# Input projections of a two-layer decoder trunk computed as three one-pass products of high and low parts

## The chip, the cores and the metric

The kernel runs on one core of a Trainium2 chip. The metric is the device time of one execution in microseconds. Three runs of the kernel before took 1989.72, 1990.03 and 1991.49 us; the median is 1990.03 us.

## The reference, cut to what matters

576 tokens (512 of a prompt, 64 of eight short decoding sequences) go through two layers. All numbers are 32-bit floats.

```
for layer in 0, 1:
    z = h @ w_in + b_in                          # 1024 -> 2072 columns
    glu(512), q(512), kv_c, kv_s, kv_w (256 each), gate(24), u_pool(256) = split(z)
    conv:  a * sigmoid(g) -> causal depthwise conv of 31 taps -> LayerNorm -> silu -> pointwise
    nsa:   q against compressed blocks (kv_c), selected blocks (kv_s), a window (kv_w),
           merged by sigmoid(gate)
    pool:  trailing-window means of u_pool, group matmul
    h = LN1(ALPHA * h + concat(conv, nsa, pool) @ w_out + b_out)
    h = LN2(ALPHA * h + FFN(h))                  # layer 0 dense, layer 1 two of eight experts
```

## The kernel before

Activations lie transposed: a tile is 128 channels (partitions) by 576 tokens, and h is eight such tiles. Every engine has its instructions in an order written out by hand, and they meet through semaphores; there is no scheduler. The names used below:

- A *product* is one output tile of 128 channels: for each of the eight k-tiles of h, a 128x128 weight tile times two halves of 288 tokens. PSUM has four pairs of banks, and the list in `schedule()` gives them out in turn: a product takes the pair of the product four places earlier and waits (in `take`) until the engine that the list names has evicted it (`z_free`).
- The input projections of a layer are 16 products: g0, g1, a0, a1 (the GLU halves), ck, cv, sk, sv, wk, wv (keys and values), p0, p1 (pooling input), q0 to q3 (queries), and one of 24 rows for the gates. They use 32-bit floats directly; the trace shows two MATMUL instructions for each half, so 32 for a product. The output projections and the dense FFN already use another form (`split_product`): weights and activations are each split into a high part (rounded to the `fp32r` type by a copy on ScalarE) and a low part (the remainder, subtracted on VectorE), and high x high, high x low and low x high are added up, one MATMUL each, 48 for a product.
- VectorE (DVE in rows) evicts a0 and a1 into `ue`, then runs the depthwise conv: 2 channel tiles x (1 + 30 taps) x (prompt, samples); the tap line is L969. Then come the pooling windows (L974 to L996), `blocks(0)` (L1021 to L1026, the eviction of the compressed-block product cmp0), and the normalization of the conv output.
- TensorE (PE) runs the 12 products g0 to p1, gate, cmp0, q0, q1, then waits for `conv_done`, then the means of the conv output (cm), q2, q3, the variances (cvar), transposes of values and gates (vt), cmp1, the pooling and pointwise products, and then the attention units.
- SyncE (SP) issues nearly all loads in one order. Before each layer's conv it issues gate weights, states and 16 cache pages, after waiting for the layer norm to be done.
- ScalarE (ACT) evicts the other products.

Weights of the input projections come in 2 MB chunks into three buffers, w0 to w2, which later hold the pieces of the output projection and the FFN.

Of the kernel before, what the change touches and what calls it, by code (L numbers as in the profile page):

```python
# [14 lines left out]
F32 = mybir.dt.float32  # L15
F32R = mybir.dt.float32r
I32 = mybir.dt.int32
ALU = mybir.AluOpType
# [32 lines left out]
NPAIR = NB // 2  # L51
SLOPE = [2.0 ** -(h + 1) for h in range(NH)]


TILES = {"glu": ("g0", "g1", "a0", "a1"), "kcks": ("ck", "cv", "sk", "sv"), "kwp": ("wk", "wv", "p0", "p1"), "q": ("q0", "q1", "q2", "q3")}
# [19 lines left out]
def schedule():  # L75
    out = [("lm", "lnc"), ("lv", "act")]
    for l in range(DEPTH):
        out += [(f"{n}.{l}", "dve" if n[0] == "a" else "act") for key in ("glu", "kcks", "kwp") for n in TILES[key]]
        out += [(f"gate.{l}", "act"), (f"cmp0.{l}", "dve"), (f"q0.{l}", "dve"), (f"q1.{l}", "dve"), (f"cm.{l}", "lnc")]
        out += [(f"q2.{l}", "dve"), (f"q3.{l}", "dve"), (f"cvar.{l}", "act")]  # L80
        out += [(f"vt{t}.{l}", "act") for t in range(5)]
# [29 lines left out]
def program(nc, a):  # L111
# [3 lines left out]
    with ctx:  # L115
# [10 lines left out]
        DHI = in_place_of_next("down_high", 4096)  # L126
        H = sb("h", KD * TOK)
# [3 lines left out]
        YT = sb("yt", KD * TOK)  # L131
        WHI = in_place_of_next("w_high", 4096)
# [62 lines left out]
        h_parts = tiles(HHI), tiles(HLO)  # L195
        mixed_parts = tiles(MHI), tiles(GLO)
# [87 lines left out]
        kc_spread = ev("kc_spread")  # L284
        piece_in = [ctx.enter_context(nc.semaphore(f"piece_in{i}")) for i in range(4)]
# [31 lines left out]
        chunk_of = {}  # L317
        for l in range(DEPTH):
            for n in ["glu", "kcks", "kwp", "cmp", "q"]:
                chunk_of[n, l] = len(chunk_of)  # L320
        NWC = len(chunk_of)

        last_read = {("glu", "a1"), ("kwp", "p1"), ("kcks", "sv"), ("q", "q3"), ("cmp", "cmp1")}
        chunk_read = {}
        for l in range(DEPTH):
            for n, z in last_read:
                chunk_read[chunk_of[n, l]] = z_full, ZI[f"{z}.{l}"] + 1


# [59 lines left out]
        def _(sp):  # L389
# [5 lines left out]
            sp.dma_start(BIAS[:, :], a["bias"]).then_inc(consts_in, 16)  # L395

            def load_w(key, src, n=4096):
                c = chunk_of[key]
                if c >= 3:
                    done, count = chunk_read[c - 3]  # L400
                    sp.wait_ge(done, count)
                if key == ("glu", 1):
                    sp.wait_ge(z_full, ZI[f"fd{KD - 1}.{NFC - 1}"] + 1)
                sp.dma_start(WR[c % 3][:, 0:n], src).then_inc(w_loaded[c % 3], 16)
# [17 lines left out]
            def load_piece(l, p):  # L422
                if p >= 4:
                    sp.wait_ge(w_low, p - 3)
                if p == pieces_start[l]:
                    sp.wait_ge(z_full, ZI[f"cmp1.{l}"] + 1)
                sp.dma_start(piece_raw[p % 4], a["split_w"][p]).then_inc(piece_in[p % 4], 16)

            for l in range(DEPTH):
                load_w(("glu", l), a["w_in"][l, 0])  # L430
                load_w(("kcks", l), a["w_in"][l, 2])
                load_w(("kwp", l), a["w_in"][l, 1])

                sp.wait_ge(ln_out, ln_done("lm" if l == 0 else "lm2"))
# [17 lines left out]
                load_w(("cmp", l), a["cmp_w"][l])  # L452
                if l == 1:
                    sp.wait_ge(z_full, ZI[f"fd{KD - 1}.{NFC - 1}"] + 1)
# [6 lines left out]
                sp.dma_start(a["out_past"][l], a["swa_cache"][l, :, TB:PAST, :]).then_inc(out_past, 16)  # L461
                for p in range(pieces_start[l], pieces_start[l] + 4):
                    load_piece(l, p)
                load_pair(l, 1)
                load_pair(l, 2)
# [71 lines left out]
        def _(pool):  # L537
# [7 lines left out]
            pool.wait_ge(consts_in, 48)  # L545
# [62 lines left out]
        def _(act):  # L608
# [40 lines left out]

            eps = SM[:, 42:43]  # L650
# [4 lines left out]
            act.wait_ge(consts_in, 48)  # L655
            norm("lm", "lv", x, h, lambda k: PAR_[:, DEPTH * NPAR + KD + k:DEPTH * NPAR + KD + k + 1])
            for l in range(DEPTH):
                for c in range(2):
                    wait_z(f"g{c}.{l}")
                    free_z(nc.scalar.activation(flat(sig[:, c, :]), pair(f"g{c}.{l}"), ACT.Sigmoid, bias=par("bin", l, c)))  # L660
                for c, name in enumerate(("ck", "cv")):
# [6 lines left out]
                    act.dma_start(a["out_kv"][l, c], kc_rows[:, c, :]).then_inc(out_kv, 16)  # L668
                for n, name in enumerate(("sk", "sv")):
                    wait_z(f"{name}.{l}")  # L670
                    free_z(nc.scalar.activation(flat(kvz[:, 2 + n, :]), pair(f"{name}.{l}"), ACT.Identity, bias=par("bin", l, 10 + n)))
                    act.dma_start(a["out_kv"][l, 2 + n], kvz[:, 2 + n, :]).then_inc(out_kv, 16)
                for n, name in enumerate(("wk", "wv")):
                    wait_z(f"{name}.{l}")
                    free_z(nc.scalar.activation(flat(kvz[:, n, :]), pair(f"{name}.{l}"), ACT.Identity, bias=par("bin", l, 4 + n)))
                    act.dma_start(a["out_kv"][l, 4 + n], kvz[:, n, :]).then_inc(out_kv, 16)
                for c in range(2):
# [4 lines left out]
                for c in range(2):  # L682
                    wait_z(f"p{c}.{l}")
                    for ps, lo, hi in pieces(f"p{c}.{l}"):
                        if hi <= SEQ:
                            done(nc.scalar.activation(ext[:, c, PW - 1 + lo:PW - 1 + hi], ps, ACT.Identity, bias=par("bin", l, 6 + c)))
                        else:
                            free_z(nc.scalar.activation(
                                ext[:, c, EP:].rearrange("p (b n) -> p b n", b=NB)[:, :, PW - 1:],
                                ps.rearrange("p (b n) -> p b n", b=NB), ACT.Identity, bias=par("bin", l, 6 + c)))  # L690
                wait_z(f"gate.{l}")
                free_z(nc.scalar.activation(flat(gT), pair(f"gate.{l}", 24), ACT.Sigmoid, bias=par("bin", l, 16, 24)))
                for a_ in range(NPAIR):
# [5 lines left out]
                    else:  # L699
                        done(ins)  # L700
                squares(f"cm.{l}", conv, 2, csq)
                deviation(f"cvar.{l}", cstd)
                for t in range(5):
                    r = P if t < 4 else NS
                    wait_z(f"vt{t}.{l}")
                    free_z(nc.scalar.activation(vg[0:r, t, :], PS[0:r, z_pair(f"vt{t}.{l}"), 0:280], ACT.Copy))
                affine(f"cm.{l}", conv, conv, 2, "clg", "clb", l, ACT.Silu)
# [66 lines left out]
                for u in range(U_L + 3):  # L774
# [11 lines left out]
                    if 4 <= u < 4 + KD:  # L786
                        m = u - 4
                        done(nc.scalar.activation(h[:, m, :], h[:, m, :], ACT.Identity, bias=par("bo", l, m), scale=ALPHA), h_scaled)
# [11 lines left out]
                if l == 0:  # L800
# [18 lines left out]
                    norm("lm2", "lv2", x, h, lambda k: par("b2", 0, k))  # L819
# [78 lines left out]
        def _(dve):  # L898
# [30 lines left out]
            def norm(lm, lv, src, g):  # L929
                center(lm, src, KD)  # L930
                dve.wait_ge(z_free["act"], freed(lv))
# [11 lines left out]
            dve.wait_ge(consts_in, 48)  # L943
            norm("lm", "lv", x, lambda k: PAR_[:, DEPTH * NPAR + k:DEPTH * NPAR + k + 1])
            for l in range(DEPTH):

                if l == 1:
                    dve.wait_ge(out_state, 16 * 8)
                for c in range(2):
                    dve.wait_ge(z_free["act"], freed(f"g{c}.{l}"))  # L950
                    wait_z(f"a{c}.{l}")
                    for ps, lo, hi in pieces(f"a{c}.{l}"):
# [3 lines left out]
                        else:  # L956
                            free_z(V.scalar_tensor_tensor(out=samples(ue[:, c, UP:])[:, :, CW - 1:], in0=samples(ps),
                                                          scalar=par("bin", l, 2 + c), in1=samples(sig[:, c, lo:hi]),
                                                          op0=ALU.add, op1=ALU.mult))

                dve.wait_ge(states_in, 16 * 5 * (l + 1))
                for c in range(2):
# [4 lines left out]
                    for k in range(1, CW):  # L967
                        for i, (out_, src) in enumerate(views):
                            ins = V.scalar_tensor_tensor(out=out_, in0=src(k), scalar=par("cw", l, c * CW + k), in1=out_,  # L969
                                                         op0=ALU.mult, op1=ALU.add)  # L970
                            (done(ins, conv_done) if k == CW - 1 and i == 1 else done(ins))

# [25 lines left out]
                def queries(j):  # L998
                    name = f"q{j}.{l}"
                    dve.wait_ge(qz_zeroed, l + 1)  # L1000
                    wait_z(name)
                    b = par("bin", l, 12 + j)
                    for ps, lo, hi in pieces(name):
                        if hi <= SEQ:
                            done(V.tensor_scalar(qp[:, j, lo:hi], ps, b, HD ** -0.5, ALU.add, ALU.mult))
                        else:
                            for g in range(NKV):
                                rows = slice(HD * g, HD * g + HD)
                                for b2 in range(2):
                                    at = b2 * HD + g * 32 + j * TB  # L1010
                                    ins = V.tensor_scalar(qs[rows, :, b2, at:at + TB],
                                                          ps[rows, :].rearrange("p (a b n) -> p a b n", a=NPAIR, b=2)[:, :, b2, :],
                                                          b[rows, :], HD ** -0.5, ALU.add, ALU.mult)
                                    (free_z if g == 1 and b2 == 1 else done)(ins)


# [12 lines left out]
                queries(0)  # L1029
                queries(1)  # L1030
                center(f"cm.{l}", conv, 2)
                queries(2)
                queries(3)
# [135 lines left out]
                dve.wait_ge(out_state, 16 * 8 * (l + 1))  # L1169
                for u in range(U_L + 4):  # L1170
# [28 lines left out]
                if l == 0:  # L1199
# [31 lines left out]
                    norm("lm2", "lv2", x, lambda k: par("g2", 0, k))  # L1231
# [161 lines left out]
        def _(pe):  # L1393
# [46 lines left out]
            def weights(key):  # L1440
                c = chunk_of[key]
                pe.wait_ge(w_loaded[c % 3], 16 * (c // 3 + 1))
                return WR[c % 3][:, :].rearrange("p (k n) -> p k n", k=KD)
# [3 lines left out]
            for l in range(DEPTH):  # L1447
                def project(key, names, normed=None):
                    w = weights((key, l))
# [471 lines left out]
```

## Time and profile before

| | us |
|---|---|
| median of three runs | 1990.03 |
| the profiled execution | 1990.08 |
| its span | 1988.5 |
| PE busy in the span | 1789.6 (90%) |
| DVE busy | 1281.2 (64%) |
| ACT busy | 906.4 (46%) |
| granted TensorE clock, mean | 0.942 of full speed |

The span is what lies between the first and the last instruction; 1.6 us lie around it. The stages of layer 0 by the start times of the trace: norm of the input until 36.5 us, projections and conv from 36.5 to 204, attention units from 204 to about 370, output projection and LN1 to about 462, dense FFN to 871, LN2 to 894; layer 1 has projections and conv from 894 to 1062, attention to 1226, output projection and LN1 to 1301, and then the experts until the end.

To read it: a busy share is an average over stages with different limits, so the stage that the change touches has to be looked at by itself, and in it which engine's end comes last at each meeting point.

### The profile page before, as it was taken

To read this page: it belongs to the slowest core of one execution; us is meant where nothing else is said; L and a number is where in the kernel's file an instruction comes from. 1 tells how busy PE (TensorE), PEld (TensorE's weight loads), DVE (VectorE), ACT (ScalarE), POOL (GpSimd) and SP (SyncE) were. 2 spreads that over 40 slices of the span, in tenths; PEclk is the share of its full clock that TensorE was granted. 3 is DMA by queue.
4 is the path that set the end of the run, shared out by engine and by line. 5 is a ranking of instruction groups with operands and counts; after the bars stand their busy time and mean duration, and the time that the engine had idled before them with its cause. 6 is when DMAs were issued, how large, how long until landed. Compare 5 with 4: busy or idle time off the path is not lost.

```text
span 1988.5 us, 27012 instructions
## 1 busy us (share of the span) xinstructions
PE 1789.6 (90%) x9941; PEld 1475.0 (74%) x9941; DVE 1281.2 (64%) x2118; ACT 906.4 (46%) x1205; POOL 51.4 (3%) x74
## 2 busy tenths in 40 slices
PE   5999788879999999979997888969999999999990
PEld 3777445769999999967775446847777777777770
DVE  4593567554444453464945675358888888888885
ACT  3021566324112212121104664148777777777772
POOL 0000000000000000000000000020000000000002
PEclk9999887799999999999998887989999999999995
DMA  6340111012222222233401011258999999999995
GB/s 248 107 128 10 64 34 34 31 64 63 78 85 74 85 85 86 64 127 113 127 14 64 22 44 49 94 213 327 367 368 365 368 367 367 367 366 368 367 367 209
DMA packets 70270, 337.10 MB, mean 170 GB/s; under 512 B 15778, under 2 KB 28770, under 8 KB 51042
## 3 DMA queue, kind: packets, MB, share of 16 engines
q1 hardware_dynamic: 61506, 308.42, 41.6%
q0 software_dynamic: 6800, 23.38, 3.4%
q10 hardware_dynamic: 1872, 4.06, 0.5%
q8 instruction: 59, 0.97, 0.2%
q14 instruction: 33, 0.27, 0.0%
HBM read 317.04 MB, written 22.85 MB: 171 GB/s over the span
## 4 chain that ended last, share of the span: by engine, by line
PE 78%; DVE 12%; issue 5%; ACT 3%; DMA 1%; SPq 0%; POOL 0%; DVEq 0%; ACTq 0%
PE ps L1632 25%; PE ps L1736 17%; PE ps L1418 15%; PE ps L1757 6%; PE ps L1564 2%; PE ps L1430 2%; PE ps L1462 2%; PE ps L1584 2%; DVE w_middle L1326 1%; DVE hidden_high L1348 1%; PE ps L1534 1%; ACT parena L737 1%; DVE parena L932 1%; PE ps L1546 1%; DVE parena L1140 1%
## 5 line engine op out<-in xcount | busy, mean ns | idle before, releaser
L1418 PE MATMUL ps<-h,w 128*128 128x288 f32 x1024 | 254.3, 412 | 15.7 <-ACT h L644 15.7
L1418 PEld LDWEIGHTS ps<-h,w 128*128 128x128 f32 x1024 | 197.2, 193 | 72.0 <-issue 17.0
L726 ACT ACTIVATE w_high<-w 128x1024 fp32r<-128x1024 f32 x82 | 87.0, 1061 | 266.1 <-PE ps L1632 264.8
L1736 PE MATMUL ps<-mixed_high,hidden_low 128*128 128x512 f32 x576 | 189.6, 400 | 3.0 <-DVE hidden_low L1331 3.0
L1736 PE MATMUL ps<-h_high,hidden_low 128*128 128x512 f32 (+1 forms) x576 | 161.1, 358 | 0.0
L1632 PE MATMUL ps<-h_high,w_low 128*128 128x288 f32 x672 | 143.9, 296 | 0.0
L1632 PE MATMUL ps<-h_low,w_high 128*128 128x288 f32 x672 | 143.9, 296 | 0.0
L1632 PE MATMUL ps<-h_high,w_high 128*128 128x288 f32 x672 | 143.9, 296 | 0.0
L839 ACT ACTIVATE mixed_high<-w 128x2048 fp32r<-128x2048 f32 x74 | 137.7, 1909 | 6.0 <-DMA w<-in_moe_gu 3.1
L1212 DVE TENSOR_TENSOR parena<-parena,ps 128x576 f32<-128x576 f32 x22 | 16.6, 754 | 186.2 <-PE ps L1632 182.3
L1632 PE MATMUL ps<-hidden_low,w_high 128*128 128x288 f32 x608 | 131.5, 297 | 0.0
L1736 PEld LDWEIGHTS ps<-mixed_high,hidden_low 128*128 128x128 f32 x576 | 109.3, 190 | 29.4 <-issue 3.2
L969 DVE SCALAR_TENSOR_TENSOR x<-uext,par,x 128x512 f32<-128x512 f32 x240 | 124.4, 518 | 8.6
L839 ACT ACTIVATE h_high<-w 128x2048 fp32r<-128x2048 f32 (+1 forms) x72 | 113.4, 1623 | 25.6 <-DMA w<-in_moe_gu 24.2
L737 ACT ACTIVATE parena<-ps 128x512 f32<-128x512 f32 (+4 forms) x136 | 69.8, 513 | 116.4 <-PE ps L1564 39.7
L1736 PEld LDWEIGHTS ps<-h_high,hidden_low 128*128 128x128 f32 x576 | 102.6, 188 | 18.1
L1348 DVE TENSOR_TENSOR hidden_high<-carena,down_high 128x2048 fp32r<-128x2048 f32 x48 | 110.0, 2292 | 1.7
L1632 PEld LDWEIGHTS ps<-h_low,w_high 128*128 128x128 f32 x672 | 108.4, 189 | 0.0
L1632 PEld LDWEIGHTS ps<-h_high,w_low 128*128 128x128 f32 x672 | 108.4, 189 | 0.0
L1632 PEld LDWEIGHTS ps<-h_high,w_high 128*128 128x128 f32 x672 | 108.3, 189 | 0.0
L1106 DVE TENSOR_TENSOR w_low<-w,w_high 128x1024 fp32r<-128x1024 f32 x82 | 100.5, 1225 | 6.7 <-ACT w_high L726 4.3
L1757 PE MATMUL ps<-down_high,hidden_low 128*128 128x512 f32 x264 | 88.3, 415 | 15.3 <-DVE hidden_high L1348 15.3
(333 smaller groups left out, 3567.2 us busy)
## 6 DMA issues: line engine op xcount, KB each, us to landing
w<-in_moe_gu SPq DMA_DIRECT2D x63, 2048.0 KB, 8.2
carena<-in_moe_dn SPq DMA_DIRECT2D x50, 1024.0 KB, 7.5
w<-in_split_w SPq DMA_DIRECT2D x82, 512.0 KB, 3.6
w<-in_w_in SPq DMA_DIRECT2D x8, 2048.0 KB, 10.7
bias<-in_moe_dn SPq DMA_DIRECT2D x13, 1024.0 KB
w<-in_moe_gu_last SPq DMA_DIRECT2D x12, 1024.0 KB, 6.9
parena<-sorted_rows POOLq DMA_DIRECT2D x12, 512.0 KB, 6.1
bias<-in_moe_dn SPq DMA_DIRECT2D x12, 512.0 KB, 9.6
```

What stands on the lines that cost most here:

```text
L726: done(nc.scalar.activation(piece_parts[p % 4][0], piece_raw[p % 4], ACT.Copy), w_high)
L737: ins = nc.scalar.activation(dst, src, ACT.Copy)
L839: nc.scalar.activation(up_high[c % 2][:, half], WR[k_ % 3][:, half], ACT.Copy).then_inc(up_high_ready, 1)
L969: ins = V.scalar_tensor_tensor(out=out_, in0=src(k), scalar=par("cw", l, c * CW + k), in1=out_, op0=ALU.mult, op1=ALU.add)
L1106: done(V.tensor_tensor(lo, piece_raw[p % 4], hi.bitcast(F32), ALU.subtract), w_low)
L1348: V.tensor_tensor(low, raw, high.bitcast(F32), ALU.subtract).then_inc(dn_low_ready, 1)
L1418: last = M(PS[0:rows, b + n, 0:HALF], w, act_[:, cols], start=(i == 0), stop=(i == len(steps) - 1))
L1430: last = M(PS[:, b + n, 0:HALF], mean[:, :], sq_[:, k % 2, cols], start=(k == 0), stop=(k == K - 1))
L1462: last = M(PS[0:HD, b, 0:2 * (NBLK + 1)], w[:, c, i, :], cmpt[:, c, :, :, i].rearrange("p b g -> p (b g)"), start=(i == 0), stop=(i == LB ...
L1632: last = M(PS[:, b + n, 0:HALF], w, act_[:, cols], start=(i == j == 0), stop=(i == len(steps) - 1 and j == 2))
L1736: last = M(PS[:, 2 + c % 2, 0:n], x_[:, k, :], w[:, k, :], start=(k == j == 0), stop=(k == KD - 1 and j == 2))
L1757: last = M(PS[:, 6 + n, :], h_, w[:, at:at + 512], start=(c == k == j == 0), stop=(c == NEC - 1 and k == last_k and j == 2))
```

## The change

- Each of the 16 input products and the gate product of a layer becomes a `split_product` of 48 MATMULs. g0 and g1 are started together (`project_first`): first all products with the high part of h, then those with the low part.
- The layer norm's ScalarE step writes h's high part (`in_parts[0]`) instead of h; eight new VectorE subtractions write the low part (`in_parts[1]`). h itself is rebuilt in the attention stage: ScalarE scales the high part (units 1 to 8 instead of 4 to 11), and eight new VectorE instructions add the low part (units 2 to 9).
- The weights come in 16 pieces of 512 KB through four raw buffers. A piece's load waits for the product four before it, its high part (ScalarE copy, three buffers) for the product three before it, its low part (VectorE subtraction, four buffers) for the high part. On VectorE pieces 0 and 1 are subtracted inside the norm, 2 to 4 after it, 5 between the evictions of a0 and a1, and 6 to 15 between conv taps, one every five.
- The first four pieces of layer 0 are loaded ahead of the 2 MB bias table, which the norm no longer waits for. The compressed-block weights come in two halves of 1 MB into the query arena.
- The evictions of q0 to q3 move from VectorE to ScalarE; the variances of the conv norm move behind the transposes of values and gates.
- In the output projection's stage the first four weight pieces are loaded after the second and third pairs of cache pages, and not before them.

The core of the diff:

```diff
+            def split_in_high(l, i):
+                n = l * IN_ALL + i
+                act.wait_ge(in_loaded[n % 4], 16 * (n // 4 + 1))
+                if i >= 3:
+                    wait_z(in_read[n - 3])
+                done(nc.scalar.activation(in_w_high[n % 3], in_raw[n % 4], ACT.Copy), in_high)
+
+            def norm_in(lm, lv, l, b):
+                squares(lm, x, KD, sq)
+                split_in_high(l, 0)
+                split_in_high(l, 1)
+                deviation(lv, std)
+                shifted(lm, x, in_parts[0], b)
+                split_in_high(l, 2)
...
+                queries(0)
+                split_in_high(l, 15)
+                queries(1)
+                queries(2)
                 squares(f"cm.{l}", conv, 2, csq)
-                deviation(f"cvar.{l}", cstd)
+                queries(3)
...
+            def split_in_low(l, i):
+                n = l * IN_ALL + i
+                dve.wait_ge(in_high, n + 1)
+                done(V.tensor_tensor(in_w_low[n % 4], in_raw[n % 4], in_w_high[n % 3].bitcast(F32), ALU.subtract), in_low)
...
+                for k in range(KD):
+                    dve.wait_ge(ln_out, ln_before["lm" if l == 0 else "lm2"][1] + k + 1)
+                    done(V.scalar_tensor_tensor(out=in_parts[1][:, k, :], in0=x[:, k, :], scalar=b,
+                                                in1=in_parts[0][:, k, :].bitcast(F32), op0=ALU.add, op1=ALU.subtract), in_h_low)
+                for i in range(2, 5):
+                    split_in_low(l, i)
...
+                    if c == 0:
+                        split_in_low(l, 5)
...
+                        taps = c * (CW - 1) + k - 1
+                        if taps % 5 == 1 and taps // 5 < IN_ALL - 6:
+                            split_in_low(l, 6 + taps // 5)
...
-                sp.wait_ge(ln_out, ln_done("lm" if l == 0 else "lm2"))
+                sp.wait_ge(in_h_low, KD * (l + 1))
                 sp.dma_start(wgate, a["w_gate"][l]).then_inc(states_in, 16)
...
-                load_w(("cmp", l), a["cmp_w"][l])
+                sp.dma_start(QA[:, 2048:4096], a["cmp_w"][l, :, 0:2048]).then_inc(cmp_in, 16)
                 sp.dma_start(poolw, a["pool_w"][l]).then_inc(mixw_in, 16)
                 sp.dma_start(pww, a["pw_w"][l]).then_inc(mixw_in, 16)
-                load_w(("q", l), a["w_in"][l, 3])
+                for i in range(4, IN_ALL):
+                    load_in(l, i)
...
-                project("q", ("q2", "q3"))
-                variances(f"cm.{l}", f"cvar.{l}", 2, MEANC, csq)
+                project("q2", "q3")
...
+                    if 2 <= u < 2 + KD:
+                        m = u - 2
+                        dve.wait_ge(h_scaled, KD * l + m + 1)
+                        done(V.scalar_tensor_tensor(out=h[:, m, :], in0=in_parts[1][:, m, :].bitcast(F32), scalar=ALPHA, in1=h[:, m, :],
+                                                    op0=ALU.mult, op1=ALU.add), h_whole)
```

On VectorE, in the second channel tile of the conv (`uext` holds its input, `x` its output), the order before is taps only:

```order
L969 SCALAR_TENSOR_TENSOR x<-uext,par,x 128x512 [waits dve_own]
L969 SCALAR_TENSOR_TENSOR x<-uext,par,x 128x64 [waits dve_own]
L969 SCALAR_TENSOR_TENSOR x<-uext,par,x 128x512 [waits dve_own]
L969 SCALAR_TENSOR_TENSOR x<-uext,par,x 128x64 [waits dve_own]
L969 SCALAR_TENSOR_TENSOR x<-uext,par,x 128x512 [waits dve_own]
```

The same place now, at the subtraction of piece 15 (L989), the last one between taps:

```order
L1042 SCALAR_TENSOR_TENSOR x<-uext,par,x 128x512 [waits dve_own]
L1042 SCALAR_TENSOR_TENSOR x<-uext,par,x 128x64 [waits dve_own]
L989 TENSOR_TENSOR w_low<-w,w_low 128x1024 [waits in_high_ready,dve_own]
L1042 SCALAR_TENSOR_TENSOR x<-uext,par,x 128x512 [waits in_low_ready]
L1042 SCALAR_TENSOR_TENSOR x<-uext,par,x 128x64 [waits dve_own]
```

Behind this subtraction 26 tap instructions (13 taps of prompt and samples) still stand before `conv_done`.

On ScalarE, at the evictions of q0 and q1 (L742 and L748, `qarena`) there is now the high part of piece 15 (L661) between them; before, no instruction of ScalarE stood there:

```order
L742 ACTIVATE qarena<-ps,bq 128x288 [waits z_full,qz_zeroed,gate_spread]
L742 ACTIVATE qarena<-ps,bq 128x224 [waits act_own]
L748 ACTIVATE qarena<-ps,bq 64x4x8 [waits act_own] x4
L661 ACTIVATE w_low<-w 128x1024 [waits z_full,in_loaded3,z_free_act]
L742 ACTIVATE qarena<-ps,bq 128x288 [waits z_full,qz_zeroed,in_high_ready]
```

The `z_full` that L661 waits for is the end of product q0, three before q3.

On TensorE, around the wait for the conv, the order before is the end of q1, the means cm, then q2:

```order
L1418 MATMUL ps<-h,w 128x288 x15
L1418 MATMUL ps<-x,meanc 128x288 [waits z_free_act,conv_done]
L1418 MATMUL ps<-x,meanc 128x288 x3
L1418 MATMUL ps<-h,w 128x288 [waits z_free_dve,w_loaded1]
L1418 MATMUL ps<-h,w 128x288 x15
```

And now:

```order
L1509 MATMUL ps<-in_high,w_middle 128x288 x2
L1480 MATMUL ps<-x,meanc 128x288 [waits z_free_act,conv_done]
L1480 MATMUL ps<-x,meanc 128x288 x3
L1509 MATMUL ps<-in_high,w_low 128x288 [waits z_free_dve,in_low_ready]
L1509 MATMUL ps<-in_high,w_low 128x288
```

The place of the two waits is unchanged; the `z_free_dve` of q2 is the eviction of cmp0 by `blocks(0)`, which VectorE reaches after the conv and the pooling windows.

## Rows read from the trace of the kernel before

**Rows 1.** The page's chain that ended last, shares of the span by engine.
```profile
PE 78%; DVE 12%; issue 5%; ACT 3%; DMA 1%; SPq 0%; POOL 0%; DVEq 0%; ACTq 0%
```

**Rows 2.** Busy time by stretch: attention of layer 0, dense FFN.
```profile
core 0: us, PE busy (x) PEld busy (x) DVE busy (x) ACT busy (x) POOL busy (x), PEclk, DMA share, GB/s
204.00:370.00 166.00, 135.90 (x736) 81.17 (x737) 109.12 (x455) 97.26 (x241) 0.00 (x0) 0.80 0.10 32
462.00:862.00 400.00, 400.00 (x3011) 400.00 (x3009) 180.56 (x210) 80.25 (x85) 0.95 (x1) 1.00 0.24 77
```

**Rows 3.** Timeline of PE, layer 0: start us, us, instructions merged.
```profile
36.52 95.01 PE L1418 MATMUL ps<-h,w 128*128 128x288 f32 x384 [7.84 <-ACT h L644]
131.46 7.94 PE L1418 MATMUL ps<-h,x 128*24 128x288 f32 x32
...
148.43 15.79 PE L1418 MATMUL ps<-h,w 128*128 128x288 f32 x64
164.05 2.10 PE L1418 MATMUL ps<-x,meanc 128*128 128x288 f32 x8
165.99 15.68 PE L1418 MATMUL ps<-h,w 128*128 128x288 f32 x64
...
186.80 9.17 PE L1462 MATMUL ps<-parena,w 128*64 128x82 f32 x64
```

**Rows 4.** Timeline of DVE, layer 0, conv to `blocks(0)`.
```profile
71.88 33.22 DVE L969 SCALAR_TENSOR_TENSOR x<-uext,par,x 128x512 f32<-128x512 f32 x60
...
139.35 0.08 DVE L974 MEMSET x<- 128x30 f32 x1
...
149.86 0.25 DVE L1026 TENSOR_SCALAR cct<-ps,sm 64x40 f32<-64x40 f32 x1
```

**Rows 5.** Timeline of the first layer norm, with idle time before and its releaser.
```profile
11.70 2.26 PE L1418 MATMUL ps<-parena,mean 128*128 128x288 f32 x4 [11.70 <-DVE parena L923]
16.37 6.28 DVE L912 TENSOR_TENSOR x<-x,ps 128x576 f32<-128x576 f32 x8 [4.81 <-DMA bias<-in_bias]
...
28.76 1.28 ACT L628 ACT_TABLE_LOAD   x1 [1.37 <-PE ps L1430]
...
34.68 6.80 DVE L934 SCALAR_TENSOR_TENSOR x<-x,par,parena 128x576 f32<-128x576 f32 x8
```

**Rows 6.** Groups by line in the dense FFN: busy us, mean ns, idle before.
```profile
L1106 DVE TENSOR_TENSOR w_low<-w,w_high 128x1024 fp32r<-128x1024 f32 x62 | 76.0, 1225 | 5.3 <-ACT w_high L726 3.5
...
L726 ACT ACTIVATE w_high<-w 128x1024 fp32r<-128x1024 f32 x62 | 65.8, 1061 | 203.5 <-PE ps L1632 202.4
```

**Rows 7.** Timeline of SP's issues around the page loads, both layers.
```profile
42.38 0.33 SPq L435 DMA_DIRECT2D x<-in_w_gate  x1
...
58.15 0.61 SPq L451 DMA_DIRECT2D parena<-in_pe  x1
...
899.85 0.33 SPq L435 DMA_DIRECT2D x<-in_w_gate  x1
...
914.26 0.62 SPq L451 DMA_DIRECT2D parena<-in_pe  x1
```

**Rows 8.** DMA issues of the whole execution: KB each, median us to landing.
```profile
w<-in_split_w SPq DMA_DIRECT2D x82, 512.0 KB, 3.6
...
w<-in_cmp_w SPq DMA_DIRECT2D x2, 2048.0 KB, 8.1
```

**Rows 9.** PE by stretch around idle times: busy, granted clock, DMA share, GB/s.
```profile
886.50:894.00 7.50, 0.01 (x1) 0.72 0.14 60
898.00:900.00 2.00, 2.00 (x6) 0.50 0.00 0
900.00:902.00 2.00, 2.00 (x10) 0.99 0.43 72
226.00:228.00 2.00, 2.00 (x10) 0.60 0.00 0
```

**Rows 10.** The chain of waits, layer 1, product cmp1.
```profile
1045.68 9.11 PE ps L1462 x64
```

**Rows 11.** Timeline of DVE in the attention stage of layer 0.
```profile
222.06 0.42 DVE L1092 CUSTOM_DVE_ANT_0 x<-con,ps 128x256 f32<-128x256 f32 x1 [3.05 <-PE ps L1549]
```

More of the change, by code:

```diff
@@ L314, in program @@
         fin_ready, out_y = ev("fin_ready"), [ctx.enter_context(nc.semaphore(f"out_y{i}")) for i in range(2)]
[L317 to L327, printed above, removed]
+        NWC = 0
+        in_read = [f"{n}.{l}" for l in range(DEPTH) for n in IN_TILES]
         pieces_of, piece_read, pieces_end = {}, [], []
@@ L1438, in norm, with split_product @@
                 variances(lm, lv, KD, MEAN, sq)
[L1440 to L1443, printed above, removed]
+            def split_product(name, steps, split=None, rows=P):
+                b = take(name)
+                for i, ((w_hi, w_lo), (a_hi, a_lo)) in enumerate(steps):
+                    if split is not None:
+                        pe.wait_ge(split[0], split[1] + i + 1)
+                    for j, (w, act_) in enumerate(((w_hi, a_hi), (w_hi, a_lo), (w_lo, a_hi))):
+                        for n, cols in halves():
+                            last = M(PS[0:rows, b + n, 0:HALF], w, act_[:, cols], start=(i == j == 0), stop=(i == len(steps) - 1 and j == 2))
+                full(last)
             pe.wait_ge(ones_set, 1)
@@ new lines, in project, with project_first @@
+                def project(*names):
+                    for name in names:
+                        w_hi, w_lo = in_weights(IN_TILES.index(name))
+                        split_product(f"{name}.{l}", [((w_hi[:, k, :], w_lo[:, k, :]), [part[:, k, :] for part in in_parts]) for k in range(KD)])
+                def project_first():
+                    first = [(f"{name}.{l}", take(f"{name}.{l}"), in_weights(i)) for i, name in enumerate(("g0", "g1"))]
+                    for k in range(KD):
+                        pe.wait_ge(ln_out, ln_before["lm" if l == 0 else "lm2"][1] + k + 1)
+                        for name, b, parts in first:
+                            for j, w in enumerate(parts):
+                                for n, cols in halves():
+                                    M(PS[:, b + n, 0:HALF], w[:, k, :], in_parts[0][:, k, cols], start=(k == j == 0), stop=False)
+                    for at, (name, b, parts) in enumerate(first):
+                        for k in range(KD):
+                            if at == 0:
+                                pe.wait_ge(in_h_low, KD * l + k + 1)
+                            for n, cols in halves():
+                                last = M(PS[:, b + n, 0:HALF], parts[0][:, k, :], in_parts[1][:, k, cols], start=False, stop=(k == KD - 1))
+                        full(last)
@@ L1463, in compress @@
                                  start=(i == 0), stop=(i == LB // 2 - 1))
                     full(last)
[L1466 to L1470 removed]
+                project_first()
+                project("a0", "a1", *TILES["kcks"], *TILES["kwp"])
@@ L1471, in _ @@
+                pe.wait_ge(gate_low, l + 1)
+                split_product(f"gate.{l}", [([part[:, k, :] for part in gate_parts], [part[:, k, :] for part in in_parts]) for k in range(KD)], rows=24)
                 pe.wait_ge(pages_in, 16 * (NB * NPG + 1) * (l + 1))
@@ L1487, in _ @@
                     full(nc.tensor.transpose(PS[0:r, b, 256:280], gT[:, cols], ident[0:24, 0:24]))
+                variances(f"cm.{l}", f"cvar.{l}", 2, MEANC, csq)
                 compress(1)
@@ L1621, in _ @@
                 pe.wait_ge(o_out, O_L * (l + 1))
-                def split_product(name, steps, split=None):
-                    b = take(name)
-                    for i, ((w_hi, w_lo), (a_hi, a_lo)) in enumerate(steps):
-                        if split is not None:
-                            pe.wait_ge(split[0], split[1] + i + 1)
-                        for j, (w, act_) in enumerate(((w_hi, a_hi), (w_hi, a_lo), (w_lo, a_hi))):
-                            for n, cols in halves():
-                                last = M(PS[:, b + n, 0:HALF], w, act_[:, cols], start=(i == j == 0), stop=(i == len(steps) - 1 and j == 2))
-                    full(last)
                 def piece(p, at):
@@ L1838, in layout @@
     gate = np.r_[1792:1816]
-    out["w_in"] = np.stack([np.stack([rows(w[:, order[n]]).reshape(P, -1) for n in ("glu", "kwp", "kcks", "q")]) for w in v["w_in"]])
+    out["w_in"] = np.stack([np.stack([rows(w[:, order[n][P * i:P * (i + 1)]]).reshape(P, -1) for n in ("glu", "kcks", "kwp", "q") for i in range(4)])
+                            for w in v["w_in"]])
     out["w_gate"] = np.stack([rows(w[:, gate]) for w in v["w_in"]])
```

155 lines of the change are left out of this document (90 added, 65 removed).

## The prediction

> **What bounds the kernel now.** I read the page's chain first: TensorE holds 78% of it, VectorE 12% [rows 1]. Where the change sits, the timeline of TensorE shows no gap: 12 products, the gate, cmp0, q0 and q1 follow each other until the means cm at 164.05 us, and cmp1 ends at 186.80 + 9.17 = 195.97 [rows 3]. VectorE's conv ends at 139.35 and `blocks(0)` at 150.1 [rows 4], so when TensorE asks for `conv_done` at 164.05 it has been there for 24.7 us, and cmp0's banks, which q2 needs, have been free for 15.9 us. TensorE bounds this stage; those two numbers are the slack that the change may use up. The stage occurs twice, once a layer.
>
> **What TensorE gains.** q0 and q1 take 164.05 - 148.43 = 15.62 us, 7.8 a product [rows 3]. The dense FFN runs the form that comes now: 3011 MATMULs in 400 us, 133 ns each [rows 2], so 48 make 6.4 us. 17 products (with the gate) save 17 x 1.4 = 24 us a layer, 48 in all, if TensorE never waits. It will, at three places.
>
> **First wait: piece 4 (for ck).** Norm of layer 0: subtracting the mean started at 16.37 because of the bias table, though its product was ready at 13.96: 2.4 us are won. Two high parts of 1.06 us [rows 6] now stand where ScalarE idled 1.37 [rows 5]: 0.75 lost, in both layers. The scaled x ends at 41.48 [rows 5], 0.9 before SP's wait ended at 42.38 [rows 7]. SP now waits for eight more VectorE subtractions of 0.85 (6.80 / 8, rows 5; the same shape and operand count). SP starts at 42.4 - 0.9 - 1.65 + 6.8 = 46.7 in layer 0 and at 899.85 - 0.9 + 0.75 + 6.8 = 906.5 in layer 1. From there to the end of the page loads it needs 58.76 - 42.38 = 16.4 and 914.88 - 899.85 = 15.0 us [rows 7], all ahead of piece 4, as are 1 MB of cmp weights and 0.375 MB of pooling and pointwise weights. 0.5 MB lands in 3.6 us and 2 MB in 8.1 [rows 8], so 2.1 + 3.0 per MB: piece 4 lands 7.7 us after the pages (bounds: 4.8, if it lands as if alone, and 9.8). High part 1.06, low part 1.23: piece 4 is ready, call it R, at 73.2 and 931.6. TensorE has done a1 at 62 (SP's 46.7, plus 0.3, 2.1 for g1's low half and 12.7 for a0, a1), so it idles 11 us, in layer 1 about 9.
>
> **Restart at the lower clock.** After 7.5 us without work [rows 9] TensorE's granted clock was 0.50 (1.2 of 2.4 GHz) until about 900 us, 6 us into the work; in the attention stage it was still so at 226, 8 us in. In half clock half the time is lost: 1.4 to 4.4 us over the restarts that I saw; I take 2.8 each (5.5 us of half clock), here and at the second stop below.
> The Trainium skill ("TensorE: Matmul & The Clock Gate", part 1) says for modelling that the ramp penalty is under 1% of a typical kernel's span and should not be fitted. By it the four restarts would be left out and the sum would be 11.2 us lower; the trace shows them, so I keep them.
>
> **Second wait: the conv.** Before piece 4 is subtracted VectorE evicts nothing: the order puts piece 4 ahead of a0. After R come a0 (1.3), piece 5 (1.23), a1 (1.3) and the taps at 33.22 / 30 = 1.107 us a pair [rows 4]. Taps and subtractions feed TensorE well enough: a product per 5 x 1.107 + 1.23 = 6.8 us against its 6.4, with a lead of 7 us that shrinks by 0.4 each. But piece 15 is subtracted behind 47 of 60 taps, due at R + 69 (3.9 evictions, 1.8 first taps, 52.0, nine subtractions 11.0, gate 0.3). Its high part has a ring of three buffers and so waits until q0 is done: R + 2.8 + 8 x 6.36 (ck to p1) + 6.36 (gate) + 9.1 (cmp0, rows 3) + 6.36 = R + 75.5, then behind q0's eviction on ScalarE (2.2, which VectorE took as well; bounds 1.5 to 3), 1.06 and 1.23. VectorE, with the 13 last taps (14.4), the pooling and `blocks(0)` queued behind, stands about 10 us. conv_done = R + 75.5 + 2.2 + 1.06 + 1.23 + 14.4 = R + 94.4: 167.6 and 1026.0. TensorE is through with q1 at R + 82 and waits 12.5 us. The whole gain up to there is gone: before, cm began at 164.05.
>
> **Third wait: q2's banks.** They are free when `blocks(0)` is done, 150.1 - 139.35 = 10.8 us after conv_done [rows 4], formerly hidden. Then q2 and q3 12.7, restart 2.8, and from q3's end to cmp1's the eviction of q3 on ScalarE ahead of the value copies (2.2), two transposes (1.1), variances 2.1 and cmp1 9.1: 14.5. Sum 40.8 from conv_done, against 195.97 - 164.05 = 31.9. cmp1 ends at 208.4 instead of 195.97 (+12.4) and at 1066.8 instead of 1045.68 + 9.11 = 1054.79 [rows 10] (+12.0). The conv norm's deviation, reciprocal and scale run beside cmp1. Behind cmp1 nothing changes.
>
> **Attention.** VectorE gets eight operations of 0.85, 6.8 us a layer, and is 66% busy there (109.12 of 166, rows 2); most of them stand at unit ends where it idles for TensorE, as 3.05 us before 222.06 [rows 11]. Bounds 0 to 6.8; I take 1.5 a layer, the two that fall where TensorE waits for a normalized tile. Moving four piece loads behind cache pages costs nothing: they are used in unit 16.
>
> **Sum.** 12.4 + 12.0 + 3 = 27.4 on the profiled execution's 1990.08 (span 1988.5 plus 1.6; the median of runs, 1990.03, is the same): 2017.5 us, 1.4% slower.
>
> **Rivals.**
> 1. *The ring of high parts is not what VectorE waits for.* Then conv_done = R + 69 + 1.2 + 14.4 = R + 84.6, 9.8 earlier a layer: 1998. For it: only 10 us decide. Against it: the order of rows on both engines leaves no way round q0. 10%.
> 2. *The other side: faster.* TensorE keeps its 24 us a layer: 1990 - 48 = 1942, or with the first wait only (11 + 9 + 5.6) 1968. Its place is the wait for `conv_done`; it decides if conv and pooling end by q1's end, R + 82. VectorE's own work after R alone is 85 us to conv_done and 95 to `blocks(0)`, so it would need piece 4 some 13 us sooner (then TensorE would come sooner too). 6%.
> 3. *Restarts cost next to nothing* (the skill's rule above): 2017.5 - 11.2 = 2006. For it: in layer 0 before, the first product was back at full clock quickly. Against it: rows 9. 10%.
> 4. *More waits.* Attention pays all of its 6.8 a layer (+10.6) and the transfers land at the late bound (+4.2): 2032. 10%.
> My forecast 60%; 4% is left for results within 0.2% by some mixture.
>
> **How the numbers follow.** The likeliest case by itself spans 2007 to 2028: landing -5.8 to +4.2, restarts -5.6 to +6.4, attention -3 to +10.6, not all on one side. For 8 in 10 I take in rivals 1 and 3, and most of 4: 1997 to 2030. This kernel can be told from no change by 0.2%, 4 us. Faster by more: 0.06 (rival 2). Within: 0.04. Slower: 0.90.
>
> **What would show it.** In the profile after: the products at 6.4 us each; TensorE idle about 11 and 9 us before ck, with VectorE's subtraction of piece 4 behind a DMA as releaser; SP's fifth weight piece issued near 64 us; VectorE idle near 10 us before its last subtraction between taps, released by ScalarE, itself released by q0; TensorE idle 12 us before cm and 6 to 9 before q2, the latter released by `blocks(0)`; a granted clock of 0.50 behind each; cmp1 of layer 0 ending near 208 us. Wrong would be: TensorE without a gap at cm; piece 4 landing before 62 us; or conv_done before q0's end.

## The result, and the profile after

The changed kernel takes 2021.89 us (median of four runs, 2020.39 to 2027.37), the kernel before, run beside it, 1989.88 us. The ratio is 1.017, 95% interval 1.0152 to 1.0188: 32 us slower. The prediction was 2017.5 us, range 1997 to 2030.

The profiled execution is the slowest of the four, 2027.37 us with a span of 2025.8, 5.5 above the median. The sums below are made against it and come to +37.3. Its span and its chain by engine:

```profile
span 2025.8 us, 28326 instructions
...
PE 71%; DVE 16%; issue 5%; ACT 4%; SPq 2%; DMA 2%; POOL 0%; DVEq 0%; ACTq 0%
```

TensorE has gone from 78% of the chain to 71%, VectorE from 12% to 16% [rows 1], SP's queue from 0% to 2%, and the DMA from 1% to 2%. The chain of layer 0 shows where (start us, us, what):

```profile
60.57 1.19 SPq L453
...
64.78 6.36 DMA w<-in_w_in
71.21 1.06 ACT w_low L661
72.36 1.24 DVE w_middle L989
73.65 59.61 PE ps L1509 x432
133.25 9.11 PE ps L1545 x64
142.36 6.60 PE ps L1509 x48
...
151.34 1.07 ACT w_low L661
152.87 1.24 DVE w_low L989
154.13 0.76 DVE x L1042
...
179.47 14.87 PE ps L1509 x96
...
201.50 9.11 PE ps L1545 x64
```

The products are as fast as hoped: ck to the gate are nine products (432 = 9 x 48) in 59.61 us, 57.6 of them at 6.4. But their chain begins with a weight piece issued behind the cache pages, and at 148.96, the end of q0, it leaves TensorE for ScalarE and VectorE. SP's queue there (start us, us, what):

```profile
46.65 0.33 SPq L440 DMA_DIRECT2D x<-in_w_gate  x1
...
49.74 12.74 SPq L453 DMA_DIRECT2D parena<-in_cmp_pages  x16
...
64.78 2.28 SPq L405 DMA_DIRECT2D w<-in_w_in  x4
```

VectorE, with idle time and releaser in brackets: it stands 19.70 us for piece 4 and 9.60 for piece 15. 26 tap instructions stand behind the latter, and then, up to `blocks(0)` (L1086), the pooling:

```profile
72.36 1.23 DVE L989 TENSOR_TENSOR w_middle<-w,w_low 128x1024 fp32r<-128x1024 f32 x1 [19.70 <-ACT w_low L661]
...
152.87 1.23 DVE L989 TENSOR_TENSOR w_low<-w,w_low 128x1024 fp32r<-128x1024 f32 x1 [9.60 <-ACT w_low L661]
154.13 14.37 DVE L1042 SCALAR_TENSOR_TENSOR x<-uext,par,x 128x512 f32<-128x512 f32 x26
168.57 0.08 DVE L1053 MEMSET x<- 128x30 f32 x1
...
179.07 0.25 DVE L1086 TENSOR_SCALAR cct<-ps,sm 64x40 f32<-64x40 f32 x1
```

What released it is on ScalarE: the eviction of q0, which waited for TensorE, then the high part of piece 15 into the buffer that q0 had been reading:

```profile
149.07 0.98 ACT L742 ACTIVATE qarena<-ps,bq 128x288 f32<-128x288 f32 x2 [13.62 <-PE ps L1509]
150.08 1.23 ACT L748 ACTIVATE qarena<-ps,bq 64x32 f32<-64x32 f32 x4
151.34 1.06 ACT L661 ACTIVATE w_low<-w 128x1024 fp32r<-128x1024 f32 x1
```

TensorE pays at three places: 10.59 us before ck (its wait for `w_middle`), 13.21 before cm, 6.71 before q2.

```profile
73.65 0.85 PE L1509 MATMUL ps<-in_high,w_low 128*128 128x288 f32 x2 [10.59 <-DVE w_middle L989]
...
168.55 4.21 PE L1480 MATMUL ps<-x,meanc 128*128 128x288 f32 x8 [13.21 <-DVE x L1042]
179.47 0.82 PE L1509 MATMUL ps<-in_high,w_low 128*128 128x288 f32 x2 [6.71 <-DVE cct L1086]
...
198.02 3.49 PE L1492 MATMUL ps<-yt,meanc 128*128 128x288 f32 x8
201.43 9.18 PE L1545 MATMUL ps<-parena,qarena 128*64 128x82 f32 x64
```

cmp1 of layer 0 ends at 210.61 and not at 195.97 [rows 3]: +14.6. By stretch (busy of PE, PEld, DVE, ACT, POOL, then the granted clock, DMA share, GB/s), the restarts before ck and before q2 begin at the lower level, a mean of 0.53 and 0.50 of full speed, and are at 1.00 from 80 and 184 us on. The variances, behind a few us of short transposes and a gap of 0.95 us, fell to 0.56:

```profile
74.00:78.00 4.00, 4.00 (x19) 4.00 (x19) 3.75 (x8) 0.79 (x1) 1.69 (x2) 0.53 0.06 18
80.00:84.00 4.00, 4.00 (x32) 4.00 (x32) 3.79 (x7) 1.26 (x2) 0.00 (x0) 1.00 0.14 32
180.00:183.00 3.00, 3.00 (x15) 3.00 (x14) 0.87 (x2) 0.00 (x0) 0.00 (x0) 0.50 0.02 5
184.00:188.00 4.00, 4.00 (x32) 4.00 (x31) 0.00 (x0) 0.00 (x0) 0.00 (x0) 1.00 0.00 0
198.00:201.00 3.00, 3.00 (x8) 2.22 (x8) 0.00 (x0) 0.80 (x2) 0.00 (x0) 0.56 0.00 0
```

Layer 1 repeats it: TensorE idles 11.78 us before ck, 12.85 before cm and 6.72 before q2. Its chain, and TensorE before its cm:

```profile
940.25 7.30 DMA w<-in_w_in
950.06 59.99 PE ps L1509 x432
...
1055.92 15.21 PE ps L1509 x96
1074.65 3.74 PE ps L1492 x8
1078.39 9.10 PE ps L1545 x64
```

```profile
1045.00 4.21 PE L1480 MATMUL ps<-x,meanc 128*128 128x288 f32 x8 [12.85 <-DVE x L1042]
```

cmp1 ends there at 1087.5, 32.7 later than in the kernel before (1054.79) [rows 10].

### The profile page after: what moved, and what is told of

Its sections match the earlier page's. It is cut to its first block, busy times and chain, and to the rows that moved or that the text cites. A ratio compares the mean times of both kernels' runs of the same rounds, so it can differ in the third digit from the quotient of the medians.

```text
span 2025.8 us, 28326 instructions
## 1 busy us (share of the span) xinstructions
PE 1766.2 (87%) x10485; PEld 1505.6 (74%) x10485; DVE 1329.5 (66%) x2136; ACT 960.6 (47%) x1289; POOL 51.0 (3%) x74
## 4 chain that ended last, share of the span: by engine, by line
PE 71%; DVE 16%; issue 5%; ACT 4%; SPq 2%; DMA 2%; POOL 0%; DVEq 0%; ACTq 0%
PE ps L1509 33%; PE ps L1808 17%; PE ps L1829 6%; PE ps L1492 2%; PE ps L1646 2%; PE ps L1545 2%; DVE w_high L1388 1%; PE ps L1480 1%; DVE hidden_high L1410 1%; DVE x L1042 1%; PE ps L1666 1%; PE ps L1616 1%; SPq L453 1%; ACT parena L794 1%; PE ps L1628 1%
## 5 line engine op out<-in xcount | busy, mean ns | idle before, releaser
L1509 PE MATMUL ps<-in_high,w_low 128*128 128x288 f32 x576 | 118.1, 304 | 35.8 <-DVE w_middle L989 22.4
L1509 PEld LDWEIGHTS ps<-in_high,w_low 128*128 128x128 f32 x576 | 92.7, 195 | 38.3 <-DVE w_middle L989 22.9
```

Source lines behind the costliest of these rows:

```text
L1509: last = M(PS[0:rows, b + n, 0:HALF], w, act_[:, cols], start=(i == j == 0), stop=(i == len(steps) - 1 and j == 2))
```

## The experiments

Each is the changed kernel with the edit shown, unless it says otherwise. The kernel before, run beside them, took 1989.46 us in the first set (the first four), 1990.37 in the second (the next three), 1989.71 in the third. Ratios are to it.

**A fourth buffer for high parts.** Piece 15's high part no longer waits for q0, and goes ahead of q0's eviction; the buffer is a part of the value-token tile, which is written later.

```diff
-                if i >= 3:
-                    wait_z(in_read[n - 3])
+                if i >= 4:
+                    wait_z(in_read[n - 4])
...
-                queries(0)
                 split_in_high(l, 15)
+                queries(0)
```

> A fourth buffer for the high parts of the weight pieces (in the value tile, which is free then), and piece 15's high part on ScalarE ahead of q0's eviction. Theory (VectorE stands for q0 before its last subtraction between taps): that wait of 9.6 us goes in both layers, conv_done comes about 85 us after piece 4 is ready and not 95, TensorE idles 3 to 4 us before cm and not 13; 19 us less in all, about 2003. Rival (VectorE's total work, not that wait, sets conv_done; or the wait turns up at the next piece): within 4 us of 2022.

Measured: 2003.55 us (2001.78 to 2005.51), ratio 1.0069 [1.0051, 1.0087]. VectorE's subtraction of piece 15 and TensorE's cm in layer 0:

```profile
142.93 1.22 DVE L990 TENSOR_TENSOR w_low<-w,v_high 128x1024 fp32r<-128x1024 f32 x1 [0.15 <-DVE x L1043]
```

```profile
158.62 3.42 PE L1481 MATMUL ps<-x,meanc 128*128 128x288 f32 x8 [3.63 <-DVE x L1043]
```

The 9.60 us are gone to 0.15, and cm comes 9.9 us earlier (158.62 for 168.55). The theory holds: 18.3 us less for the 19 expected. The run changes two things at once, the size of the ring and the place of piece 15's high part; with three buffers the high part would wait for q0 in any place. How the 9.6 us divide is shown by a later run, which has q0's eviction out of the way and still three buffers (the query evictions back on VectorE, below): 7.69 us of the wait are left there. So the ring makes up 7.7 of the 9.6 us and the eviction ahead of the high part 1.9.

**`blocks(0)` right behind the conv taps**, ahead of the pooling windows, so that q2 finds its banks free:

```diff
+                blocks(0)
+
                 dve.wait_ge(ln_out, ln_done("lm" if l == 0 else "lm2"))
...
-                blocks(0)
```

> VectorE evicts cmp0 right behind the conv taps, ahead of the pooling windows. Theory (q2 waits for cmp0's banks): TensorE goes from cm to q2 without its 6.7 us of idle time, and restarts once instead of twice; 8 to 9 us less a layer, about 2005. Rival (q2 to q3 are not on the path, since the conv norm behind the pooling windows ends later anyway): within 4 us of 2022.

Measured: 2003.86 us (2000.01 to 2006.73), ratio 1.0074 [1.0056, 1.0091]. cm is where it was, TensorE goes on to q2 without a gap, and cmp1 ends at 200.9:

```profile
168.75 4.21 PE L1481 MATMUL ps<-x,meanc 128*128 128x288 f32 x8 [13.21 <-DVE x L1042]
...
189.57 2.21 PE L1493 MATMUL ps<-yt,meanc 128*128 128x288 f32 x8
191.71 9.18 PE L1546 MATMUL ps<-parena,qarena 128*64 128x82 f32 x64
```

So the third wait was worth 18.0 us, as the theory had it (8 to 9 a layer). The variances run at full clock here, 2.21 us and not 3.49. That need not be the wait's doing: in the second profile of the changed kernel (the last run below) they also took 2.21 us in layer 0, with the wait in place.

**Pieces 4 and 5 issued ahead of the cache pages:**

```diff
+                load_in(l, 4)
+                load_in(l, 5)
                 for b in range(NB):
...
-                for i in range(4, IN_ALL):
+                for i in range(6, IN_ALL):
```

> SP issues weight pieces 4 and 5 ahead of the 16 cache pages, not behind them. Theory (piece 4 is what holds TensorE before ck and VectorE before a0): piece 4 is ready before a1 is done, TensorE has no gap before ck (10.8 us in layer 0, about 10 in layer 1, with a restart of some 2 to 3 us each); the rest of the chain shifts with it; 13 us less a layer, about 1995. Rival (the pages or pieces 6 and 7 behind them become what is late): half of it or less, 2008 or more.

Measured: 2005.46 us (2002.35 to 2007.69), ratio 1.0077 [1.0057, 1.0097]; between the two. The gap before ck is gone, but the next piece, 6, is still behind the pages, and VectorE now stands for it, with all later taps behind:

```profile
74.21 1.23 DVE L991 TENSOR_TENSOR w_middle<-w,w_low 128x1024 fp32r<-128x1024 f32 x1 [6.47 <-ACT w_low L663]
...
142.49 1.23 DVE L991 TENSOR_TENSOR w_low<-w,w_low 128x1024 fp32r<-128x1024 f32 x1 [5.35 <-ACT w_low L663]
```

conv_done moved 10.4 us, from 168.55 to 158.18. A load can be early enough for TensorE and the next one late for VectorE; I had followed only the first.

**The eight VectorE additions in the attention stage left out** (h then keeps only its high part, scaled):

```diff
-                        done(V.scalar_tensor_tensor(out=h[:, m, :], in0=in_parts[1][:, m, :].bitcast(F32), scalar=ALPHA, in1=h[:, m, :],
-                                                    op0=ALU.mult, op1=ALU.add), h_whole)
```

> The eight VectorE operations a layer that add h's low part back in the attention stage are left out (so h keeps only its high part there). Theory (they fall into VectorE's idle time but for two): 3 us less, 2019. Rival (VectorE bounds the attention stage, each counts): 13.6 us less, 2008.

Measured: 2021.43 us (2020.99 to 2022.06), ratio 1.0156 [1.0139, 1.0173], the changed kernel's time within 0.5 us. The additions cost nothing that can be measured. VectorE is busy for 117.7 us of the attention stage of layer 1 with them and 111.6 without, and the stage takes 176.2 and 176.9 us; so they fall where VectorE has time to spare.

**All three edits together** (the ring of four, `blocks(0)` first, pieces 4 and 5 first).

> The three edits together: four buffers for high parts, blocks(0) right behind the conv taps, weight pieces 4 and 5 ahead of the cache pages. Theory (the three waits stand one after another on one path): their gains add, 18.3 + 18.0 + 16.4 = 53 less than 2021.9, about 1970, below the kernel before. Rival (they hide one another, since VectorE's own work of about 85 us behind a1 becomes the bound): 1985 or more.

Measured: 1979.61 us (1970.01 to 1981.65), ratio 0.9924 [0.9895, 0.9954]. The three alone gave 18.3, 18.0 and 16.4, together 52.7; combined they gave 42.3. So they are three waits and not one, and this version is faster than the kernel before. But the time lies between the theory (about 1970) and the rival (1985 or more), and the trace shows part of the rival's mechanism. VectorE no longer stands for piece 15 (0.15 us), but it still stands 6.46 us for piece 6, and the taps behind it end later than TensorE is done with q1:

```profile
152.42 3.78 PE L1484 MATMUL ps<-x,meanc 128*128 128x288 f32 x8 [8.02 <-DVE x L1045]
```

Also, one of the four executions took 1970.01 us and the three others 1978.8 to 1981.7, so the 42.3 is not known to the last few us.

**The same, with piece 6 issued between the two halves of the pages:**

```diff
                 for b in range(NB):
+                    if b == NB // 2:
+                        load_in(l, 6)
...
-                for i in range(6, IN_ALL):
+                for i in range(7, IN_ALL):
```

> As the one with all three edits, and piece 6 issued in the middle of the page loads. Theory (with pieces 4 and 5 ahead, VectorE stood 6.5 us at its first subtraction between taps for piece 6, which still came behind the pages; that is why moving pieces 4 and 5 gave 16 us and not 27): another 6 to 6.5 us a layer, about 1958. Rival (the shortfall lies in the page loads being later): no change against the kernel with three edits.

Measured: 1965.74 us (1961.35 to 1968.95), ratio 0.9867 [0.9844, 0.989]: 13.9 less than without piece 6, for the 12 to 13 of the theory; the 1958 was counted from the 1970 that the version without piece 6 had not reached. This is the fastest version, 24.6 us under the kernel before of its set. It is not the 48 us of the products. cmp1 of layer 0 ends 14.2 us sooner than in the kernel before (181.8 for 195.97), not 24: TensorE still waits 6.87 us for the conv, and cm takes 2.1 us more at the lower clock; in layer 1 the wait is 4.21. VectorE still stands for a piece, now piece 7. And behind cmp1 of layer 1 some 7 us of the gain are lost, 4.1 of them in the attention stage (see below).

```profile
77.75 1.23 DVE L994 TENSOR_TENSOR w_low<-w,v_high 128x1024 fp32r<-128x1024 f32 x1 [3.45 <-ACT v_high L666]
```

```profile
149.39 4.21 PE L1486 MATMUL ps<-x,meanc 128*128 128x288 f32 x8 [6.87 <-DVE x L1047]
...
992.08 4.21 PE L1486 MATMUL ps<-x,meanc 128*128 128x288 f32 x8 [4.21 <-DVE x L1047]
```

**The query evictions back on VectorE** (the changed kernel otherwise):

```diff
-                queries(0)
                 split_in_high(l, 15)
-                queries(1)
-                queries(2)
...
                 blocks(0)
+                queries(0)
+                queries(1)
                 center(f"cm.{l}", conv, 2)
+                queries(2)
+                queries(3)
```

> The changed kernel with the evictions of q0 to q3 put back on VectorE behind blocks(0), as before. Theory (in the changed kernel q0's eviction of 2.2 us on ScalarE stands between q0 and piece 15's high part, on the path): conv_done 2.2 us sooner in both layers and the four evictions hidden beside q2 and q3: 2017.5. Rival (on VectorE they stand between blocks(0) and the conv norm's mean subtraction and hold the bank that the transposes need): 2022 to 2030.

Measured: 2012.78 us (2007.17 to 2017.01), ratio 1.0106 [1.0079, 1.0134]. The direction was right, the size double: 9.1 and not 4.4. Piece 15 is subtracted 2.0 us sooner, since ScalarE has no eviction ahead of its high part:

```profile
150.83 1.23 DVE L967 TENSOR_TENSOR w_low<-w,w_low 128x1024 fp32r<-128x1024 f32 x1 [7.69 <-ACT w_low L661]
```

In layer 0 cmp1 ends 4.0 us earlier (206.6): 2.0 are this, and 1.3 are the variances, at full clock here (2.21 us), which the second profile of the changed kernel shows too. From piece 4 to cmp1's end the gain is 3.9 us in layer 0 and 4.7 in layer 1; what goes beyond 2.0 a layer is less time at the lower clock, as in the nine products behind piece 4 of layer 1 (58.05 us for 59.99). Whether the edit brings that is not shown.

**The same edit on top of the fastest version.**

> This is the kernel with all four edits (ring of four high parts, blocks(0) behind the conv, pieces 4 and 5 ahead of the cache pages and piece 6 between them; 1965.7 us), and the evictions of q0 to q3 go back to VectorE, behind blocks(0) and around the subtraction of the mean. In the changed kernel by itself that edit was worth 9 us. Theory: it gained there because ScalarE reached the high part of piece 15 earlier and VectorE stood 1.9 us less, and because the high ring was the wait; with four high buffers and piece 15 ahead of q0 there is nothing left to win in that place, conv_done stays at 149.4 us in layer 0, and the time is within 4 us of 1965.7. Rival: VectorE is the better engine for the eviction whatever the ring (the value copies behind q3 start earlier on ScalarE): cmp1 of layer 0 ends 2 to 4 us before 181.8 and the time is 1956 to 1961.

Measured: 1967.08 us (1964.88 to 1977.60), ratio 0.99 [0.9867, 0.9933], 1.3 above the fastest version and within the 4 us of the theory. One part of the theory was wrong: conv_done came at 146.4 and not 149.4, because piece 7 arrived 3 us sooner (VectorE stood 0.38 us for it). Nothing in the edit touches that load, so this is not to the edit's credit. TensorE gave that back before q3, in a wait for q0's banks: their eviction stands behind the conv and the pooling on VectorE:

```profile
146.42 3.70 PE L1487 MATMUL ps<-x,meanc 128*128 128x288 f32 x8 [3.71 <-DVE x L1025]
159.52 0.67 PE L1516 MATMUL ps<-in_high,v_high 128*128 128x288 f32 x2 [3.02 <-DVE qarena L1086]
```

So with the ring wider, no difference can be seen between the evictions on ScalarE and on VectorE.

**The changed kernel once more, nothing edited.**

> The changed kernel once more, nothing edited, for a second profile. In the first profile the time from the output projection to the FFN of layer 0 was 92.0 us, where four of the variants had 89.7 to 90.0, and the norm ahead of layer 1 ran at a granted clock of 0.74. If that is a matter of when the granted clock falls and rises in one execution, the second profile of the same program differs from the first by 2 to 6 us in these stages and ends near 2021. If it belongs to the program, both profiles show 92.0 and 0.74.

Measured: one execution, 2026.98 us. The stage from the output projection to the FFN took 477.18 - 385.20 = 91.98 us again, and the norm ahead of layer 1 ran at 0.76. For these two stages the first alternative did not come about, and the time did not end near 2021. But two executions are few, and two other places did differ between the profiles of this same program: the variances of layer 0's conv norm took 3.49 and 2.21 us (cmp1 ended 2.0 us earlier), and the variances of the norm between output projection and experts in layer 1 took these times, first and second profile:

```profile
1322.06 8.47 PE ps L1492 x32
```

```profile
1320.99 10.91 PE ps L1492 x32
```

## Why the prediction was right, point by point

- **What bounds the kernel, and the gain in the products:** confirmed. The pitch of the products is 6.4 us.
- **First wait:** confirmed. SP started at 46.65 (predicted 46.7) and piece 4's subtraction ended at 73.6 (73.2). TensorE idled 10.59 (11). In layer 1 R (the moment when piece 4 is ready) is 950.0; with the 15.1 us handed down by layer 0 taken off it is 934.9, not 931.6, and TensorE idled 11.78 (about 9). Of these 3.3, 1.2 are SP's start (922.79 - 15.1 for 906.5), of which 1.05 are the variances of the norm behind the FFN (11.19 us for 10.14 before); 0.8 are the page loads (15.8 us to their end for 15.0); and 1.2 are the landing of piece 4, 8.9 us behind the pages for 7.7. In layer 0 that landing took 8.0. Both landings lie within the forecast's bounds of 4.8 to 9.8.
- **Restarts:** the four that I had put at 2.8 each took 2.0 and 2.4 before ck (59.61 and 59.99 against 57.6), 2.1 and 2.4 at q2 (14.87 and 15.21 against 12.8): 8.9 for 11.2. But the variances behind q3 fell to the lower clock too, 3.49 and 3.8 us for 2.10, which I hadn't counted. With them the restarts come to 12. In the second profile the four are 1.6, 2.7, 1.8 and 2.6, and only layer 1's variances are longer (1.7), so 10.4 in all. Rival 3 (they cost next to nothing) is refuted by these rows.
- **Second wait:** confirmed, VectorE stood 9.60 and 9.63 us (about 10), q0's eviction on ScalarE took 2.24 (2.2), conv_done came at 168.55 (167.6). Rival 1 (the ring is not the wait) is refuted by the fourth buffer: with it and piece 15 ahead of q0's eviction the wait is 0.15 us. TensorE waited 13.21 (12.5).
- **Third wait:** confirmed, 6.71 (6 to 9), and from conv_done to cmp1's end 42.1 us (40.8); the variances' 1.4 make the difference. cmp1 ended at 210.6 (208.4).
- **Attention:** this term was mis-sized. I took 1.5 us a layer for the eight additions, 3 in all; without them the median is 0.5 us lower, which is within the spread of the runs. The stage itself, from cmp1's end to the output projection, takes 175.3 and 176.2 us for 177.2 and 172.1 before, but without the additions it takes 176.9 twice, so the 4.1 us more in layer 1 are not theirs. There the kernel before had a mean granted clock of 0.84 and the changed one of 0.80; in all the variants it was 0.78 to 0.81, and the stage took 175.2 to 179.7. Rival 4 is refuted in its attention half.
- **"Behind cmp1 nothing changes"** failed in one place: the stage from the output projection to the FFN of layer 0 took 92.1 us for 89.7, by the clock in its norm (last section).
- **The sum.** Predicted 12.4 + 12.0 + 3 = 27.4. In the profile it is 14.6 (layer 0) - 1.9 (attention) + 2.4 (to the FFN) + 17.6 (layer 1) + 4.1 (attention) + 0.5 = 37.3; by the medians 32.0. In the profile of the kernel without the additions, whose median is the same, layer 1 adds only 11.9 (1082.5 - 1054.8, less the 15.7 handed down); piece 4 is ready 4.6 us sooner there (946.1 - 15.7 for 934.9), 2.7 of it because the variances behind the FFN took 8.46 us and not 11.19. The forecast's 12.0 is at that end. So part of the miss of the profile, and the closeness of the median to the forecast, hang on how those norms fell, which the forecast said nothing of. Why both profiled executions of the changed kernel (2027.37, 2026.98) are 4 to 7 us longer than its three others (2020.39 to 2022.60), while those of the variants are not, stays open. Both have the longer form of two norms, together 5.2 us more than the version without the additions; whether the others have the shorter one no run shows.

Rival 2 (faster) did not come about. But its condition, piece 4 sooner and the conv done in time, is what the combined versions go towards, and at 1979.6 and 1965.7 us they end on its side.

## What to carry to other kernels

When products get cheaper, add up what the other engine does from the first operand's arrival to the meeting point, the waits in the middle of its queue included: here the 24 us a layer that the forecast worked out for TensorE became 10.6, 13.2 and 6.7 us of waiting. A ring of buffers whose last refill waits for a late consumer stalls everything queued behind the refill. One more buffer, with the refill ahead of an eviction, gave 18 us; so did the eviction of cmp0 a few places earlier. Waits behind one another can still be separate, and still not add up in full (42.3 of 52.7 here): undo each alone, then all together.

## What the runs showed of the hardware that was not expected

The 32 variance MATMULs of the norm between output projection and FFN have two durations, by the clock they are granted. In the changed kernel, and in the version without the additions:

```profile
444.50:455.00 10.50, 10.50 (x31) 7.30 (x32) 4.42 (x6) 4.73 (x7) 0.00 (x0) 0.75 0.10 41
```

```profile
446.70:455.00 8.30, 8.28 (x32) 5.49 (x32) 4.44 (x6) 4.76 (x7) 0.00 (x0) 1.00 0.13 51
```

10.93 us at a clock of 0.75 or 8.46 at 1.00, though the two programs differ only in the attention stage ahead. In layer 0 both profiles of the changed kernel show the long form (10.93 and 10.89), and the version with a fourth buffer alone and the one with three edits have it too; but in layer 1 the same norm of the same program had the short form in the first profile and the long one in the second. So it does not simply go with the program. The norm behind the FFN varies too: 11.19 and 11.18 us in the changed kernel, 10.14 before, 8.46 with `blocks(0)` first, 9.93 with four high buffers. The Trainium skill ("TensorE: Matmul & The Clock Gate", part 1) says that how many matmuls run at the lower clock differs from run to run of one kernel; the norm of layer 1 bears that out here, while that of layer 0 was the same in the two profiles of one version and differed between versions. What decides it no run here shows. It bounds what a comparison of stages can tell: 2.5 us a norm, and 2.7 for the norm behind the FFN.
